# Modulation columns of a two-network block: one copy and one turn for every four blocks instead of for every one

## The reference, cut to what matters

```python
def mod_vectors(cvec, w_mod, b_mod):
    m = jax.nn.silu(cvec) @ w_mod + b_mod          # (1024,) @ (1024, 9216) + (9216,)
    return jnp.split(m, N_MOD, axis=-1)            # nine vectors of 1024

def modulate(h, shift, scale):
    return h * (1.0 + scale) + shift

def sandwich_ffn(x, w_gate_up, w_down, g_pre, g_post, shift, scale, gate):
    h = modulate(rms_norm(x, g_pre), shift, scale)
    return x + 0.5 * gate * rms_norm(swiglu(h, w_gate_up, w_down), g_post)

for l in range(2):
    mx, mc = mod_vectors(c, w_mod[l], b_mod[l]), mod_vectors(c_ctx, w_mod[l], b_mod[l])
    # ffn with mx[0:3] / mc[0:3], attention mix with [3:6], second ffn with [6:9]
```

## Time and profile before

| | us |
|---|---|
| median of 3 runs | 3363.03 (3361.87 to 3368.07) |
| the profiled execution, its own time | 3360.89 |
| its span | 3358.5 |
| PE busy in the span | 3108.9 (93%) |
| DVE busy | 1706.7 (51%) |
| ACT busy | 1377.6 (41%) |
| POOL busy | 216.4 (6%) |
| mean granted PE clock | 0.951 of full |

### The profile page before, as it was taken

One profiled execution on the slowest core, in us unless ns is written; L12 is line 12 of the kernel. 1 busy time (PEld: TensorE's weight loads), 2 busy tenths in 40 slices (PEclk: granted clock), 3 DMA queues, 4 the chain that ended last, 5 costly groups with the idle time before them and its releaser, 6 DMA issues. The chain is left out here.

```text
span 3358.5 us, 53925 instructions
## 1 busy us (share of the span) xinstructions
PE 3108.9 (93%) x21948; PEld 2741.9 (82%) x21948; DVE 1706.7 (51%) x2624; ACT 1377.6 (41%) x2238; POOL 216.4 (6%) x304
## 2 busy tenths in 40 slices
PE   6999989789999899997889889997799999989998
PEld 4777858567777688886789889997599999978998
DVE  3332253553322533235655557655575677556765
ACT  3222232532222332224445455544364546444644
POOL 1111014201111000011300000000000000000000
PEclk8999989989999899998989999998799999999999
DMA  7555344025554232253235543544155455543453
GB/s 256 176 163 163 110 126 128 26 98 166 175 169 146 88 100 95 93 160 114 78 117 194 161 156 114 188 152 133 38 176 188 160 170 176 189 142 122 152 195 106
DMA packets 405775, 474.88 MB, mean 141 GB/s; under 512 B 10860, under 2 KB 383164, under 8 KB 405578
## 3 DMA queue, kind: packets, MB, share of 16 engines
q1 hardware_dynamic: 380176, 389.05, 35.9%
q0 software_dynamic: 24544, 82.74, 7.9%
q10 hardware_dynamic: 858, 0.29, 0.0%
HBM read 470.84 MB, written 4.84 MB: 142 GB/s over the span
## 5 line engine op out<-in xcount | busy, mean ns | idle before, releaser
L423 DVE TENSOR_TENSOR w_lo<-w_raw,w_hi 128x1024 fp32r<-128x1024 f32 x734 | 898.4, 1229 | 1298.5 <-ACT w_hi L420 1297.4
L431 PE MATMUL bank<-a_hi,w_hi 128*128 128x256 f32 (+1 forms) x3864 | 1245.6, 322 | 69.7 <-DVE a_lo L1363 16.4
L432 PE MATMUL bank<-a_lo,w_hi 128*128 128x256 f32 (+1 forms) x3864 | 1231.9, 319 | 0.0
L433 PE MATMUL bank<-a_hi,w_lo 128*128 128x256 f32 (+1 forms) x3864 | 1229.5, 318 | 0.0
L420 ACT ACTIVATE w_hi<-w_raw 128x1024 fp32r<-128x1024 f32 x734 | 771.3, 1056 | 1018.5 <-PE bank L433 998.8
L431 PEld LDWEIGHTS bank<-a_hi,w_hi 128*128 128x128 f32 x3864 | 746.2, 193 | 147.3 <-issue 81.7
L433 PEld LDWEIGHTS bank<-a_hi,w_lo 128*128 128x128 f32 x3864 | 743.9, 193 | 50.8
L432 PEld LDWEIGHTS bank<-a_lo,w_hi 128*128 128x128 f32 x3864 | 745.0, 193 | 48.0
L431 PE MATMUL bank<-h_hi,w_hi 128*128 128x256 f32 (+1 forms) x1728 | 544.7, 315 | 0.0
L432 PE MATMUL bank<-h_lo,w_hi 128*128 128x256 f32 (+1 forms) x1728 | 540.0, 313 | 0.0
L433 PE MATMUL bank<-h_hi,w_lo 128*128 128x256 f32 (+1 forms) x1728 | 539.5, 312 | 0.0
(11 more groups left out here) (287 smaller groups left out, 2436.7 us busy)
## 6 DMA issues: line engine op xcount, KB each, us to landing
w_raw<-in_mlp_w SPq DMA_DIRECT2D x128, 1024.0 KB, 5.3
w_raw<-in_w_ffn_gate_up SPq DMA_DIRECT2D x88, 1024.0 KB, 5.2
m_raw<-in_w_mod POOLq DMA_DIRECT2D x128, 512.0 KB, 4.8
w_raw<-in_w_ffn_down SPq DMA_DIRECT2D x32, 1024.0 KB, 6.7
w_raw<-in_gla_w_in SPq DMA_DIRECT2D x24, 1024.0 KB, 5.3
w_raw<-in_w_in SPq DMA_DIRECT2D x16, 1024.0 KB, 5.8
w_raw<-in_ple_w_gate SPq DMA_DIRECT2D x16, 1024.0 KB, 5.1
w_raw<-in_w_ffn_down SPq DMA_DIRECT2D x16, 768.0 KB, 5.6
```

What stands on the lines that cost most here:

```text
L423: e.tensor_tensor(lo, raw, hi.bitcast(F32), ALU.subtract).then_inc(S.lo_ready.sem, 1)
L431: e.matmul(dst, hi, rhs_hi, start=start, stop=False)
L432: e.matmul(dst, hi, rhs_lo, start=False, stop=False)
L433: return e.matmul(dst, lo, rhs_hi, start=False, stop=stop)
```

## The change

Four blocks in a row accumulate side by side in one bank. The two live columns of `c_pad` move from places 0 and 1 to places 6 and 7 of each 32, and block r of a batch (r = 0 to 3) multiplies with the columns from 2r on, 32 - 2r of them. Its results then land 6 - 2r partitions behind the start of each column group. Only the first matmul of block 0 opens the accumulation; the zeros in the other columns add nothing to the neighbours. After the fourth block (or the last of a shorter batch) DVE copies once and PE turns once, against a `mod_sum` of eight columns; the output goes to bank 7 with pairs of columns four apart. The bias is added by one DVE instruction for the whole batch, where ACT had two per block. The matrix `mod_sum` grows from 8 to 32 bytes per partition; in the built program each other buffer keeps its address. Blocks, loads and their places in the loops stay.

```diff
+MOD_BATCH = 4
-    c["mod_sum"] = np.tile(np.eye(P // 4, 2, dtype=np.float32), (4, 1))
+    c["mod_sum"] = np.tile(np.eye(P // 4, 2 * MOD_BATCH, dtype=np.float32).reshape(P // 4, MOD_BATCH, 2)[:, ::-1].reshape(P // 4, -1), (4, 1))
...
+            def batch_of(j, per):
+
+                q = j // MOD_BATCH
+                return q, j % MOD_BATCH, min(MOD_BATCH, (j // per + 1) * per - MOD_BATCH * q), -(-per // MOD_BATCH)
+
             def mod_rows(i, j, per):
...
-                b, count = bank[4 + j % 2][:, 0:SC], S.mod_rows.n + j
-                own = count - FIRST_MODS
+                q, r, size, batches = batch_of(j, per)
+                b, count, batch = bank[4 + q % 2][:, 0:SC], S.mod_used.n // 2 + j, S.mod_rows.n + q
+                own, skip = count - FIRST_MODS, 2 * r
...
                     if pe:
-                        if half == 0 and count > 1:
-                            e.wait_ge(S.mod_rows.sem, val(count - 1, i, per))
+                        if half == 0 and r == 0 and batch > 0:
+                            e.wait_ge(S.mod_rows.sem, val(batch, i, batches))
...
-                            mm = e.matmul(b[32 * g:32 * g + 32, :], c_pad[:, k0 + g, :], src[:, g, :], start=half == 0, stop=half == 1)
+                            mm = e.matmul(b[32 * g:32 * g + 32 - skip, :], c_pad[:, k0 + g, skip:], src[:, g, :],
+                                          start=r == 0 and half == 0, stop=r == size - 1 and half == 1)
                         mm.then_inc(S.mod_used.sem, 1)
+                if dve and r == size - 1:
+                    e.wait_ge(S.mod_used.sem, val(2 * count + 2, i, 2 * per))
+                    if batch > 0:
+                        e.wait_ge(S.mod_turned.sem, val(batch, i, batches))
+                    e.tensor_copy(at.rows[:, q % 2, :], b).then_inc(S.mod_rows.sem, 1)
+
+            def mod_turn(i, j, per):
+
+                q, r, size, batches = batch_of(j, per)
+                if r != size - 1:
+                    return
+                t = (at.mod_layer * MOD_SLOTS + at.mod_slot + MOD_BATCH * q) * 2
+                n = 2 * size
+                b, batch = bank[7][:, 0:2 * n], S.mod_rows.n + q
+                if pe:
+                    e.wait_ge(S.mod_rows.sem, val(batch + 1, i, batches))
+                    if batch > 0:
+                        e.wait_ge(S.mod_done.sem, val(batch, i, batches))
+                    for m in range(2):
+                        mm = e.matmul(b.rearrange("p (r m s) -> p m r s", m=2, s=2)[:, m, :, :], at.rows[:, q % 2, m * P:m * P + P],
+                                      mod_sum[:, 0:n], start=True, stop=True)
+                    mm.then_inc(S.mod_turned.sem, 1)
                 if dve:
-                    e.wait_ge(S.mod_used.sem, val(2 * count + 2, i, 2 * per))
-                    if count > 1:
-                        e.wait_ge(S.mod_turned.sem, val(count - 1, i, per))
-                    e.tensor_copy(at.rows[:, j % 2, :], b).then_inc(S.mod_rows.sem, 1)
-
-            def mod_turn(i, j, per):
...
-                    for m in range(2):
-                        mm = e.matmul(b[:, 2 * m:2 * m + 2], at.rows[:, j % 2, m * P:m * P + P], mod_sum[:, :], start=True, stop=True)
-                    mm.then_inc(S.mod_turned.sem, 1)
-                if act:
-                    e.wait_ge(S.mod_turned.sem, val(count + 1, i, per))
-                    for m in range(2):
-                        e.activation(part(mod[:], 2 * (t + m), i, 4 * per, 2), b[:, 2 * m:2 * m + 2], ACT.Identity,
-                                     bias=part(cols[:], COL["b_mod"] + t + m, i, 2 * per, 1)).then_inc(S.mod_done.sem, 1)
+                    e.wait_ge(S.mod_turned.sem, val(batch + 1, i, batches))
+                    pairs = lambda x: x.rearrange("p (t s) -> p t s", s=2)
+                    e.tensor_tensor(pairs(part(mod[:], 2 * t, i, 4 * per, 2 * n)), pairs(b),
+                                    part(cols[:], COL["b_mod"] + t, i, 2 * per, n).unsqueeze(2).to_broadcast([P, n, 2]),
+                                    ALU.add).then_inc(S.mod_done.sem, 1)
...
-                    e.activation(c_pad[:, :, 0], vec("c", 0, DK), ACT.Silu).then_inc(S.act.sem, 1)
-                    e.activation(c_pad[:, :, 1], vec("c_ctx", 0, DK), ACT.Silu).then_inc(S.act.sem, 1)
+                    e.activation(c_pad[:, :, 2 * MOD_BATCH - 2], vec("c", 0, DK), ACT.Silu).then_inc(S.act.sem, 1)
+                    e.activation(c_pad[:, :, 2 * MOD_BATCH - 1], vec("c_ctx", 0, DK), ACT.Silu).then_inc(S.act.sem, 1)
```

More of the change, by code:

```diff
@@ L247, in build @@
         c_pad = sb("c_pad", [P, DK, P // 4])
-        mod_sum = sb("mod_sum", [P, 2])
+        mod_sum = sb("mod_sum", [P, 2 * MOD_BATCH])
         stat = sb("stat", [P, 24])
@@ L521, in mods_done @@
-            def mods_done(count):
+                if dve and r == size - 1:
[18 more added lines that the diff above has]
+                    mm.then_inc(S.mod_turned.sem, 1)
+                if dve:
+                    e.wait_ge(S.mod_turned.sem, val(batch + 1, i, batches))
[3 more added lines that the diff above has]
+                                    ALU.add).then_inc(S.mod_done.sem, 1)
@@ L522, in mods_done @@
+            def mods_done(count, batches):
                 S.mod_used.n += 2 * count
-                S.mod_rows.n += count
-                S.mod_turned.n += count
-                S.mod_done.n += 2 * count
+                S.mod_rows.n += batches
+                S.mod_turned.n += batches
+                S.mod_done.n += batches
                 at.mod_slot += count
@@ L538, in mods @@
                 rep(passes, body, loads=True)
-                mods_done(passes * per)
+                mods_done(passes * per, passes * batch_of(0, per)[3])
             def mod_vec(layer, chunk):
@@ L609, in gemm @@
                 if mod_per:
-                    mods_done(mod_per * pairs)
+                    mods_done(mod_per * pairs, pairs // per * batch_of(0, per * mod_per)[3])
             def hidden_at(flat, p, m, i, per, n):
@@ L683, in gate_up @@
                 if mod_per:
-                    mods_done(mod_per * pairs)
+                    mods_done(mod_per * pairs, -(-pairs // per))
             def to_z(n, add=False):
```

## The result

| | before | changed |
|---|---|---|
| median, us | 3361.87 (3354.7 to 3368.07, 5 runs) | 3330.48 (3323.64 to 3337.93, 5 runs) |
| the profiled execution, its own time | 3360.89 | 3327.05 |
| its span | 3358.5 | 3324.9 |

The ratio is 0.9899, its 95% interval 0.9881 to 0.9917. The direction and the mechanism were forecast; the time lies 1.5 us under the range of 3332 to 3350 and 10.5 under the forecast of 3341.

The account below looks back on a forecast made before the run. The prediction took PE, busy without waits, to bound the loops, and a chain of PE, DVE and ACT the start. Its terms, 15.3 + 1.1 + 0.3 + 5.0 = 21.7 us, gave 3341 us, range 3332 to 3350.

Parts of the forecast that it names:

- What bounds the kernel: In the loops PE is always busy, so each PE instruction costs its distance to the next start.
- Term 1: Loops, 45 turns removed behind a product: 0.34 us each, 15.3 us in all; upper bound 19.4.
- The narrower weight loads: Rows of blocks with 30, 28 or 26 columns instead of 32: no visible saving, bound 0.
- Term 2: The two turns removed behind a column sum: at least 0.54 us each, 1.1 us in all.
- Term 3: End of the first ffn: two ACT activations ahead of the squares PE waits for go to DVE, 0.3 us.
- Term 4: Program start, first eight blocks: DVE begins w_lo at 44.4 instead of 49.38; gain 5.0 us, range 2.7 to 7.4.
- Block 8's load: Program start: this load is issued some 4 us earlier and is not late; DVE's own chain is next in line.
- 1 (0.43 a turn): Loops: the tile step costs nothing, so a removed turn saves all 0.43 us; 19.4 us there, 3337 total; chance 10%.
- 2 (something else holds the loops): Weight loads or ACT's cut hold the loops, PE only waits longer; total 3357 or 3358 us; chance 5%.
- 3: Remaining turns: strided output slows them; at a doubled 0.43, 7.3 us come back, total 3348; chance 6%.
- 4: Rows under 32 columns: a pass's four matmuls run one after another, 138 us more, total 3479; chance 4%.
- 5: Buffers: the wider mod_sum moves a neighbour and changes other instructions' times; no time assigned; chance 1%.

Follow-up runs that it names:

- dummy_turn: Changed kernel with two idle matmuls of the old turn's form put back behind each block that lost its turn; median 3351.69 us, ratio 0.9976 to before.
- wide32: Changed kernel, but each block's rows use 32 columns again, read across a k-tile's end; median 3338.28 us, ratio 0.9927 to the kernel before.
- ctl_after: The changed kernel unchanged, run again as a second sample; median 3337.99 us, ratio 0.9938 to the kernel before.
- ctl2_after: The changed kernel unchanged, run once more on another chip; median 3329.65 us, ratio 0.9903 to the kernel before.

## Why the forecast was right in kind and 10 us off in size

- **What bounds the kernel**: right. PE's time is the price in the loops: `dummy_turn` gives back 1.01 of the 1.16 us of four slots with PE's instructions alone.
- **Term 1, 15.3, came out as 45 x 0.385 = 17.3.** The step from products to rows is 0.32 as read from one place, and with 32 columns a mid-batch slot wins exactly 0.340; over all 45 turns this step brought 15.4. **The term that failed is the one of the products beside it**: "The narrower weight loads (30, 28, 26 columns) save nothing I can see: bound 0", and with it the silent assumption that 48 products take as long as before. They took 1.8 us less over the loops. `wide32` shows that 0.9 of it, 0.025 per turn, is the narrower operand; the other 0.02 per turn stay in `wide32` and in `dummy_turn`, so neither the width nor the missing turn makes them, and their cause is open. The same part explains the two signs that were missed by a little: a mid-batch slot of 12.10 to 12.12 where 12.14 was forecast, a batch's last slot of 12.45 where 12.48 was.
- **Term 2, 1.1, was 2 x 0.67 = 1.3**: I had counted only the turn, and not the wider step from the sum to it, which goes as well.
- **Term 3, 0.3**: ACT's squares follow its cut by 1.25 before and by 0.97 now, 0.28 less (before's two rows first, has what stands between):

```profile
464.42 1.06 ACT L420 ACTIVATE w_hi<-w_raw 128x1024 fp32r<-128x1024 f32 x1 [2.96 <-PE bank L433]
465.67 1.15 ACT L777 ACTIVATE tmp_g<-z 128x512 f32<-128x512 f32 x2
450.73 1.06 ACT L421 ACTIVATE w_hi<-w_raw 128x1024 fp32r<-128x1024 f32 x1 [2.96 <-PE bank L434]
451.70 1.13 ACT L791 ACTIVATE tmp_g<-z 128x512 f32<-128x512 f32 x2
```

  The leads between 455 and 480 us grow by 0.3 to 1.2 in the three traces of the changed kernel; what makes them more than 0.28 isn't shown, and I take 0.5 in the sum.
- **Term 4, 5.0**: 5.0 in the first trace, 4.2 as mean of three traces of each kernel, and 4.9 by the second slot, since the clock comes back sooner behind the first product. That the sum of this term held is partly luck, as two errors cancel: the clock gave some 0.6 where nothing was taken for it, and one step was wrong. "Block 8's load is issued some 4 us earlier too and is not what is late": it is what is late next. In `ctl_after`, the first row is its issue on POOL:

```profile
41.38 1.55 POOL L492 DMA_DIRECT2D m_raw<-in_w_mod  x2 [16.23 <-PE bank L503]
...
48.77 0.48 DVE L922 SCALAR_TENSOR_TENSOR a_lo<-z,mod,a_hi 128x256 fp32r<-128x256 f32 x1
49.25 1.08 PE L503 MATMUL bank<-m_raw,c_pad 128*32 128x256 f32 x8 [6.93 <-DMA m_raw<-in_w_mod]
...
50.90 1.08 PE L503 MATMUL bank<-m_raw,c_pad 128*32 128x256 f32 x8 [0.57 <-DMA m_raw<-in_w_mod]
51.91 0.80 PE L432 MATMUL bank<-a_hi,w_hi 128*128 128x512 f32 x1
```

  The first product comes 3.14 behind the first a_lo, where it follows by 1.37 in the first traces of both kernels (55.71 to 57.08, 51.40 to 52.77): the second half of the load, issued at 42.2, can be used only at 50.9, 8.7 us later, beside other loads (the mean busy share of the DMA engines in between is 1.07), where the kernel before waited 4.7 us for it at a share of 0.68 (issued at 47.2, used at 51.9). It is issued 5 us earlier and usable only 1.0 earlier, in the other two traces of the changed kernel 0.4 and 0.5. Here that gives 1.8 us back, in `ctl2_after` 0.8.
- **The sum** by place is then 4.9 + 17.3 + 1.3 + 0.5 = 24.0, and the traces' leads at 1731 us say 24.2. The forecast had 21.7. This is the part of the error that has a place in the kernel, 2.3 us, most of it the 2.0 that term 1 lacked.
- **The other step that failed is the range.** "The runs of before spread over 6 us, and the median of others may lie 2 us off": three runs say little of the spread. 87 runs of the same kernel go from 3346 to 3374, and with a deviation of 6 the median of five is good to some 3 us, that of two such sets to 5. Of the 10.5 us by which the result lies under the forecast, 2.3 are the terms and 1.2 are that the median of before came out at 3361.87 and not 3363.03; the other 7 no differing instruction explains. With two such deviations the range would have had to reach 10 us to either side of a sum that was itself 2 us off; it reached 9.
- **Rivals.** 1 (0.43 a turn) falls: the step costs 0.09, and 0.385 comes about otherwise. 2 (something else holds the loops) falls with 24.40 of 24.40 us busy. 3 falls: turns with eight columns in pairs four apart hold the same 0.43 (0.435 where two columns held 0.430); the rule of the Trainium skill ("PSUM — Partial Sum Buffer", Specifications (TRN2)) that a non-contiguous pattern slows matmuls doesn't show in this form. 4 falls: rows of 26 to 30 columns take 1.00. 5 has nothing for it: DVE's 734 cuts take 898.2 us where they took 898.4, and in the second network, which would feel a moved neighbour, the traces show no gain that goes with the change.

## What to carry to other kernels

On an engine that is always busy, price an instruction by the distance between its neighbours with and without it, and look whether the neighbours change too: here the operand became narrower and the products behind it a little quicker, and a step at the other side of the turn went as well. Elsewhere in the same kernel the shorter work only uncovers the next wait, here a load that no one had waited for. And before giving a range, ask how the untouched parts behave from one execution to the next: match the instructions of two traces and look at the lead where nothing differs.

## What the runs showed of the hardware

**Two paces.** With no idle time and the clock fully granted, a stream of matmuls of 256 columns runs at 113 or at 118 ns per matmul, and holds one of the two over many weight slots of 48 matmuls: 25 slots from 1731 us on, 19 from 2074 on. In such stretches the pace differs from execution to execution of the same program; others are alike in all twelve traces, as the seven slots from 2563 us on, always slow. It differs in the first network's last part as in the second (443 or 444 against 427 matmuls in 50 us; 532 against 512 in 60). One such stretch makes 4 to 5 us; in ten traces (both first results and the first eight experiments) what the slower pace adds to the second network sums to 10 to 22 us, and this sum goes with most of the spread of its time, 1418 to 1434 us. What chooses the pace isn't shown. The streams of 512 columns, 0.227 to 0.23 apart, show no such step: 48 of them take 10.83 us or 0.03 to 0.04 less.

**The price of a change of the tile** shows as 0.09 us at the entry (0.32 instead of 0.23 behind a product of 512 columns) and about 0.31 from the last group of four rows to the first product, where the groups themselves stand 0.22 apart. With a short turn between products and rows the way is 0.66; without it 0.34 less, and not the 0.43 that the turn seems to hold.
